# Who computes the low halves, and what VectorE does in which order, in a two-layer hybrid transformer kernel with experts

## The reference

```python
for l in range(DEPTH):                                   # DEPTH = 2
    u = rms_norm(x, norm_mix[l]) @ w_in[l]               # four mixers on slices of u, then
    y = rms_norm(stack([mla, pool, swa, conv]), ...)     # a norm by group
    x = x + y @ w_mix_out[l]
    m = rms_norm(mem, norm_mem[l])                       # 256 memory tokens
    x = x + cross_attention(rms_norm(x, norm_xa[l]), m, ...)
    x = x + hier_moe(rms_norm(x, norm_ffn[l]), ...)

def hier_moe(t):          # 4 groups of 8 experts, D_EXPERT = 256
    g_idx = argmax(g_logits)                             # one group for a token
    top_p, top_i = top_k(softmax(e_logits[rows, g_idx]), 2)   # two experts of it
    # 1024 (token, expert) pairs sorted by expert; for each expert's rows xb:
    y = (silu(xb @ w_gate[e]) * (xb @ w_up[e])) @ w_down[e]
    # y * weight is added back to its token
```

## Time and profile before

| | before |
|---|---|
| median of 3 runs | 1306.23 us (1302.16 to 1306.77) |
| the profiled execution: its time, its span | 1300.3 us, 1298.6 us |
| TensorE busy | 1185.5 us, 91% |
| VectorE busy | 702.1 us, 54% |
| ScalarE busy | 350.5 us, 27% |
| GpSimd busy | 68.8 us, 5% |
| the chain that ended last | PE 80%, DVE 11%, issue 3%, ACT 2%, DVEq 2%, DMA 1%, ACTq 1% |
| mean granted TensorE clock | 0.954 |

### The profile page before, as it was taken

One profiled execution on the slowest core, in us unless ns is written; L12 is line 12 of the kernel. 1 busy time (PEld: TensorE's weight loads), 2 busy tenths in 40 slices (PEclk: granted clock), 3 DMA queues, 4 the chain that ended last, 5 costly groups with the idle time before them and its releaser, 6 DMA issues.

```text
span 1298.6 us, 17523 instructions
## 1 busy us (share of the span) xinstructions
PE 1185.5 (91%) x5132; PEld 636.9 (49%) x5132; DVE 702.1 (54%) x1592; ACT 350.5 (27%) x737; POOL 68.8 (5%) x125
## 2 busy tenths in 40 slices
PE   5999999999396999999889998999994699999996
PEld 3754555556362444444457555555663444444443
DVE  3345664567763555555642365545766635555554
ACT  3215221124512222222232242210335122222221
POOL 8000000000206000000000000000002000000000
PEclk8999999999698999999989999989996989999999
DMA  9040024400404999999342200244013069999991
GB/s 291 18 130 1 1 65 130 195 1 2 195 0 148 421 416 418 423 421 422 153 140 66 65 1 1 66 130 195 1 40 156 0 243 409 418 422 422 419 382 65
DMA packets 52102, 243.15 MB, mean 187 GB/s; under 512 B 7872, under 2 KB 18400, under 8 KB 26944
## 3 DMA queue, kind: packets, MB, share of 16 engines
q1 hardware_dynamic: 48816, 238.30, 46.4%
q0 software_dynamic: 2688, 1.91, 0.9%
q10 hardware_dynamic: 528, 2.10, 0.4%
HBM read 240.19 MB, written 2.10 MB: 187 GB/s over the span
## 4 chain that ended last, share of the span: by engine, by line
PE 80%; DVE 11%; issue 3%; ACT 2%; DVEq 2%; DMA 1%; ACTq 1%
PE ps L2507 17%; PE ps L2117 10%; PE ps L2540 9%; PE ps L2336 8%; PE ps L2109 7%; PE ps L2491 6%; PE ps L2492 4%; PE ps L2087 4%; PE ps L2138 4%; PE ps L2384 2%; PE ps L2179 2%; PE ps L2477 1%; PE ps L2391 1%; PE ps L2187 1%; DMA X<-in_x 1%
## 5 line engine op out<-in xcount | busy, mean ns | idle before, releaser
L2507 PE MATMUL ps<-wgu,xw 128*64 128x512 f32 x1024 | 228.3, 599 | 18.8 <-ACTq L1184 17.7
L1958 DVE TENSOR_TENSOR X<-ps,X 128x512 f32<-128x512 f32 x256 | 155.9, 680 | 10.9 <-issue 9.0
L2117 PE MATMUL ps<-hT,ring 128*128 128x512 f32 x352 | 157.0, 601 | 0.0
L2507 PEld LDWEIGHTS ps<-wgu,xw 128*64 128x64 f32 x1024 | 75.6, 139 | 165.9 <-issue 165.9
L2540 PE MATMUL ps<-wdn,hhT 128*64 128x512 f32 x512 | 119.7, 610 | 2.8 <-ACTq L1202 2.8
L2336 PE MATMUL ps<-ring,yT 128*128 128x512 f32 x256 | 117.9, 609 | 0.4 <-DVE X L1361 0.4
L2491 PE MATMUL ps<-yhi,Wt 128*128 128x512 f32 x256 | 114.0, 445 | 3.7 <-DVEq L1247 3.7
L2117 PEld LDWEIGHTS ps<-hT,ring 128*128 128x128 f32 x352 | 66.6, 193 | 77.4 <-issue 77.4
L2492 PE MATMUL ps<-ylo,Wt 128*128 128x512 f32 x256 | 101.0, 394 | 0.0
L1976 DVE SCALAR_TENSOR_TENSOR ylo<-ps,ws,yhi 128x512 fp32r<-128x512 f32 x64 | 48.0, 750 | 73.5 <-ACTq L1212 73.5
L1965 DVE TENSOR_TENSOR hh<-ps,silu 128x256 f32<-128x256 f32 x32 | 13.6, 424 | 134.8 <-ACTq L1190 134.8
(11 more groups left out here) (373 smaller groups left out, 1550.4 us busy)
## 6 DMA issues: line engine op xcount, KB each, us to landing
wgu<-in_w_gate SPq DMA_DIRECT2D x64, 1024.0 KB, 8.0
wgu<-in_w_up SPq DMA_DIRECT2D x64, 1024.0 KB, 10.2
wdn<-in_w_down SPq DMA_DIRECT2D x64, 1024.0 KB, 10.6
ring<-in_w_in SPq DMA_DIRECT2D x8, 1024.0 KB, 6.7
ring<-in_w_mix_out SPq DMA_DIRECT2D x12, 512.0 KB, 5.8
w_kv<-in_xa_w_kv SPq DMA_DIRECT2D x2, 2048.0 KB, 9.5
ring<-in_w_in SPq DMA_DIRECT2D x2, 2048.0 KB, 17.1
ring<-in_w_in SPq DMA_DIRECT2D x2, 1536.0 KB, 20.2
```

The costliest lines, as they stand in the source:

```text
L1958: tt(xh, bank, xh, ALU.add).then_inc(mfreed((what, n)), 1)
L2117: last = mm(bank, w[:, c, c0:c0 + P], hT[:, c, :], start=c == 0, stop=c == KD - 1)
L2507: last = mm(bank[r], xw[:, c, r], wgu[2 * parity + j][:, :, c, :], start=c == 0, stop=c == KD - 1)
```

## The change

The diff, cut to what the text speaks of:

```diff
@@ SyncE @@
                 sp.dma_start(w_kv[:], cols("xa_w_kv", l, 0, 512)).then_inc(w_kv_in, 16)
+                with sp.If(l < 1):
+                    sp.dma_start(X[:], x_d).then_inc(x_in, 16)
@@ GpSimd @@
...
+            pool.affine_select(out=ident[:], in_=ident[:], ...)
+            pool.drain()
+            pool.nop().then_inc(ident_ready, 1)
...
-                load_gain(3, "norm_mem", gains_in)
-                load_gain(0, "norm_mix", gains_in)
...
-                for t in range(NT):
-                    wait_apart(pool, S["xhi_ready"], done(l, "xhi_ready", t + 1))
-                    pool.tensor_tensor(xlo[:, t], xs[:, t], xhi[:, t].bitcast(F32), ALU.subtract)
@@ ScalarE @@
-            act.wait_ge(mem_in, 16)
-            act.dma_start(X[:], x_d).then_inc(x_in, 16)
+            load_gains(0)
...
+                with act.If(l > 0):
+                    load_gains(l)
                 act.wait_ge(S["layer_done"], l + 1)
...
-                    chunked = X[:, t].rearrange("p (j c) -> p c j", c=KD)
-                    copy(xs[:, t].rearrange("p (c j) -> p c j", c=KD), chunked, scale=rstd_x[:, t:t + 1])
-                    copy(xhi[:, t].rearrange("p (c j) -> p c j", c=KD), chunked,
-                         scale=rstd_x[:, t:t + 1]).then_inc(S["xhi_ready"], 1)
+                    copy(xhi[:, t], X[:, t], scale=rstd_x[:, t:t + 1]).then_inc(S["xhi_ready"], 1)
...
+                act.wait_ge(S["rank_read"], done(l, "rank_read", 1))
+                copy(rt[:, 0:2].rearrange("p a b -> p (a b)")[:, 0:NT * NE + NE],
+                     ps[:, dense.job["rank",][0], 0:NT * NE + NE]).then_inc(freed(("rank",)), 1)
+                act.nop().then_inc(S["rank_kept"], 1)
@@ VectorE @@
+            def first_of(vals, n, m, code, tmp):
+                for t in range(NT):
+                    stt(tmp[:, t], vals[:, t], m[:, t:t + 1], descending[:, 0:n], ALU.is_equal, ALU.mult)
+                dve.drain()
+                nc.vector.tensor_reduce(code.unsqueeze(2), tmp, AX_X, ALU.max)
...
+                def low_part(t):
+                    dve.wait_ge(S["xhi_ready"], done(l, "xhi_ready", t + 1))
+                    stt(xlo[:, t], X[:, t], rstd_x[:, t:t + 1], xhi[:, t].bitcast(F32), ALU.mult, ALU.subtract)
+                    signal("xlo_ready")
...
                 one_hot(0, 0)
+                low_part(0)
                 one_hot(0, 1)
-                dve.nop().then_inc(S["starts_ready"], 1)
+                low_part(1)
+                ts(dest_2[:], dest[:], -float(SEQ), None, ALU.add)
+                nc.vector.tensor_copy(starts[:], row(4))
+                signal("starts_ready")
+                low_part(2)
                 one_hot(0, 2)
+                low_part(3)
                 one_hot(0, 3)
+                token_weights()
+                one_hot(1, 0)
+                sorted_gain(0)
+                one_hot(1, 1)
+                tiles_past()
+                one_hot(1, 2)
                 padded_places()
-                one_hot(1, 0)
-                one_hot(1, 1)
-                sorted_gain(0)
-                one_hot(1, 2)
                 one_hot(1, 3)
-                overflow_tiles()
-                token_weights()
                 nc.vector.memset(xgT[:, :, 2 * SEQ:SORTED], 0.0)
                 sorted_gain(1)
                 placed()
+                overflow_tiles()
                 step_(0, 0, False)
@@ TensorE @@
-            pe.wait_ge(init_pool, 1)
+            pe.wait_ge(ident_ready, 1)
...
+                pe.wait_ge(S["rank_kept"], done(l, "rank_kept", 1))
...
-                                mm(mbank_of(l, 0, ("sorted", half, c)), xhi[:, t, c * P:(c + 1) * P], hot,
+                                mm(mbank_of(l, 0, ("sorted", half, c)), xhi[:, t, c::KD], hot,
...
-                                mm(bank, xhi[:, t, c * P:(c + 1) * P], hot, start=False, stop=False)
-                            last = mm(bank, xlo[:, t, c * P:(c + 1) * P], hot, start=False, stop=t == NT - 1)
+                                mm(bank, xhi[:, t, c::KD], hot, start=False, stop=False)
+                            last = mm(bank, xlo[:, t, c::KD], hot, start=False, stop=t == NT - 1)
```

More of the change, by code:

```diff
@@ L449, in build @@
         xw = at("xw", [P, KD, P], F32, late + 4096)
+        passed = at("passed", [P, OVF, NE], F32, late + 8192)
+        begun = at("begun", [P, OVF, NE], F32, late + 10240)
         W1 = at("W1", [P, SEQ], F32, late + 12288)
@@ L483, in build @@
         past = small("past", [P, 8])
+        descending = small("descending", [P, NE])
         kTx = small("kTx", [P, 2, MEM])
@@ L502, in build @@
         ssq_q = small("ssq_q", [P, NT])
-        eps_q = small("eps_q", [P, 1])
         lg = small("lg", [P, NT, 36])
@@ L863, in square, with load_gains @@
                 return nc.scalar.activation(dst, src, ACT.Square, **kw)
-            act.wait_ge(mem_in, 16)
-            act.dma_start(X[:], x_d).then_inc(x_in, 16)
+            def load_gains(l):
+                for i, name in ((3, "norm_mem"), (0, "norm_mix")):
+                    act.dma_start(gains[:, i, :], lay(name, l).rearrange("l (p c) -> p (l c)", c=KD),
+                                  allow_slow_non_contiguous=True).then_inc(gains_in, 16)
+            load_gains(0)
             act.wait_ge(rope_arg, 1)
@@ L930, in _ @@
             with act.Fori(0, DEPTH) as l:
+                with act.If(l > 0):
+                    load_gains(l)
                 act.wait_ge(S["layer_done"], l + 1)
+                act.wait_ge(mem_in, (l + 1) * 16)
+                for i in range(NM):
+                    square(xn[:, i], memx[:, i], accum_out=mem_s[:, 0, i:i + 1])
+                    act.drain()
+                act.nop().then_inc(S["mem_ssq"], 1)
                 act.wait_ge(x_in, 16)
@@ L937, in _ @@
                 act.nop().then_inc(S["x_ssq"], 1)
-                act.wait_ge(mem_in, (l + 1) * 16)
-                for i in range(NM):
-                    square(xn[:, i], memx[:, i], accum_out=mem_s[:, 0, i:i + 1])
-                    act.drain()
-                act.nop().then_inc(S["mem_ssq"], 1)
                 normalise(l, 0)
@@ L1384, in _ @@
                 dve.sem_inc(s_, 1)
-            dve.wait_ge(init_pool, 1)
+            for j in range(16):
+                freq = float(np.float32(THETA) ** (-np.float32(j) / np.float32(16)))
+                nc.vector.memset(freqs[:, j:j + 1], freq)
+            nc.vector.memset(ovf_f[:], 0.0)
+            nc.vector.memset(ssqY[:], 1.0)
+            for w in range(4):
+                rows = slice((w % 2) * HALF, (w % 2 + 1) * HALF)
+                nc.vector.memset(inv_w[rows, w // 2:w // 2 + 1], 1.0 / WINDOWS[w])
+                nc.vector.memset(inv_n[rows, w // 2, :], float(WINDOWS[w]))
             dve.wait_ge(pos_in, 16)
@@ L1440, in _ @@
                 signal("mem_rstd")
+                stream_rstd(l, 0)
                 for t in range(NT):
@@ L1772, in _ @@
-                tt(r32(1), lg[:, :, NG:36], rstd_x[:].unsqueeze(2).to_broadcast([P, NT, NE]), ALU.mult)
+                for t in range(NT):
+                    stt(lg[:, t], lg[:, t], rstd_x[:, t:t + 1], b_rt[:], ALU.mult, ALU.add)
                 dve.drain()
-                tt(r4(0), r4(0), b_rt[:, 0:NG].unsqueeze(1).to_broadcast([P, NT, NG]), ALU.add)
-                tt(r32(1), r32(1), b_rt[:, NG:36].unsqueeze(1).to_broadcast([P, NT, NE]), ALU.add)
+                nc.vector.tensor_reduce(r1(3), groups, AX_X, ALU.max)
@@ L1846, in sorted_gain, with tiles_past @@
                         signal("xgT_dve")
-                def padded_places():
+                def tiles_past():
+                    dve.wait_ge(S["rank_kept"], done(l, "rank_kept", 1))
                     past_7 = over[:, 0:NE * 7].rearrange("p (e k) -> p e k", k=7)
@@ L1852, in padded_places @@
                        past[:, 0:7].unsqueeze(1).to_broadcast([P, NE, 7]), ALU.is_gt)
+                    nc.vector.memset(row(2), 0.0)
                     dve.drain()
@@ L1860, in padded_places @@
                     stt(row(2), row(3), float(NE - 1), iota[:, 0:NE], ALU.add, ALU.subtract)
+                def padded_places():
                     ts(r32(5), rank, float(SLOTS), None, ALU.is_ge)
```

145 lines of the change are left out of this document (60 added, 85 removed).

## The result

| | before | after |
|---|---|---|
| median (range), runs | 1306.5 us (1302.16 to 1308.18), 4 | 1268.62 us (1267.95 to 1269.59), 4 |
| span of the profiled execution | 1298.6 us | 1267.9 us |
| mean granted TensorE clock | 0.954 | 0.966 |
| first routing operation to first expert product, layer 0 / 1 | 66.24 / 66.17 us | 48.38 / 48.31 us |

The changed kernel takes 0.9719 of the time of the one before, 95% interval 0.9691 to 0.9748. It is 37.9 us faster on the medians. The forecast was 1257 us from a gain of 46.4; the time is within its range of 1246 to 1276 but 11.6 us above the forecast. On the two profiled spans only 30.7 us are seen; experiment 12 tells where the rest went.

What follows compares the result with a forecast made beforehand. The prediction took TensorE, 91% busy and waiting for VectorE in sorting, as the bound. Gains of 4.1 (start), 21.2 and 21.1 us (layers) sum to 46.4, between 1253.9 and 1259.8: 1257 us, range 1246 to 1276.

Steps and rivals of the forecast that it cites:

- GpSimd's stalls: In routing and sorting, four VectorE operations a layer are held while GpSimd uses SBUF; removing this saves 8.55 us.
- The order: VectorE evicts right behind its last G: 5.6 us less at the halves' turn, expert-step gap 3.5 instead of 9.
- M to the first product: From the matrix M to the first sorting product: 7.2 us less, of which 6.46 are stalls.
- strided weight loads taken as 0: TensorE's 256 sorting weight loads in steps of 8 elements fit beside products of 0.227 us and cost 0.
- rival A: Strided loads slow the sorting products by up to 0.095 us each, 24 us in all: 1281; chance 0.06.
- The top-two chain, "0.8 less": From the first routing operation to M: shorter scalings, top-two steps and group part save 0.8 us, besides a 2.09 stall.
- The start, 4.1 us: At the kernel's start, earlier gains and X landing at 18.7 bring the third tile to 32.3 instead of 36.41.
- The level: Whole-kernel base for the gain: profiled run 1300.3 gives 1253.9, median 1306.23 gives 1259.8; 1257 taken.
- B: VectorE's long routing operations are not GpSimd's doing, so 8.5 us stay in each layer: 1274; chance 0.06.
- D: Expert steps are bound by DMA and give back what sorting gains, 42 us: 1299; chance 0.02.
- C: The start gives nothing, X being as late behind `w_kv` as beside it: 1261; chance 0.04.
- E: Strided loads are not hidden beside sorting products, 256 times, 82 us: 1339, slower than before; chance 0.02.

Runs made afterwards that it cites:

- experiment 12: The kernel before, unaltered, profiled again: 1303.5 us, ratio 0.9993.
- experiment 3: The changed kernel with the low halves worked out by GpSimd again, from an extra copy by ScalarE: 1282.52 us, ratio 0.9833.
- experiment 4: The kernel before with only the low halves moved to VectorE and TensorE's weight loads strided; old order, chain and start kept: 1295.14 us, ratio 0.9943.
- experiment 5: The changed kernel with VectorE's old order behind the fourth low half and the overflow list in its old, longer form: 1288.62 us, ratio 0.988.
- experiment 9: The changed kernel, but GpSimd asks for its small parameters only when X has landed: 1264.82 us, ratio 0.97.
- experiment 6: The changed kernel with the old start (gains by GpSimd's queue, one constants signal, X asked for by ScalarE, X's squares first): 1272.45 us, ratio 0.9744.
- experiments 2 and 10: The changed kernel with halves laid out by chunks for contiguous weight loads: for all token tiles 1266.73 us, for tiles 1 to 3 only 1270.43 us.

## Why the prediction was right, and where it missed

The time fell within the range and the two main mechanisms held; the forecast of the gain was 8.4 us too high, and one of the prediction's own signs of being wrong, products spaced wider than 0.24, came true. The rows add up: 17.86 us from routing to experts in either layer and 2.33 at the start are 38.0, and 1306.5 - 38.0 = 1268.5, near the measured 1268.62. That it meets so closely is luck: the interval of the ratio is 3.7 us either way, and the clock in the mixers moves a profile by more. The forecast had 46.4.

- **GpSimd's stalls: right.** Put back into the changed kernel (experiment 3) they cost 7.0 and 6.9 us a layer; the held operations there begin later within GpSimd's 2.36 us than those of the earlier trace rows, whose surplus was 8.55. With only this edit (experiment 4) the gain is 4.8 and 4.1: in layer 0 about 1.6 went to the first low half, for which TensorE waited, and 2.3 to strided loads.
- **The order: right.** 8.8 and 9.2 us a layer by experiment 5, the longer list included. No wait at the turn but 0.24; the gap ahead of the expert step 3.44 us (forecast 3.5).
- **M to the first product: right**, 3.79 us where 342.4 - 338.55 = 3.85 was worked out; the low part took 1.28 us (1.4 taken), and VectorE stayed ahead. The overflow list is hidden: it begins at 384.90, beside gate and up.
- **The step that failed most, strided weight loads taken as 0.** I compared eight strided transposes with eight contiguous ones and concluded that a strided load fits. A transpose's load is not that of a sorting product: here the trace shows 330 ns against 188. There was a warning in the profile of before, in its weight loads of those transposes, which I had not read (contiguous `Prx`, then strided `X`):
```profile
L2087 PEld LDWEIGHTS ps<-ident,Prx 128*128 128x128 f32 x64 | 7.5, 143 | 1.5 <-issue 1.1
L2087 PEld LDWEIGHTS ps<-ident,X 128*128 128x128 f32 x128 | 16.2, 194 | 3.9 <-issue 2.3 <-ACT PTx L860 1.1 <-DVEq L1247 0.3
```
  The spacing of the transposes does not show these 51 ns. The half's 64 products take 0.245 x 64 = 15.7 us, not 14.5, so the two halves take 33.75 us together in layer 0 and 33.88 in layer 1 instead of the forecast 31.4: 2.4 a layer (128 x 0.018 = 2.3). This is rival A's mechanism at a fifth of its bound: 0.018 us a product and not 0.095, 4.6 us and not 24. The load is 0.14 us longer and the spacing 0.018, so the rest lies beside the product ahead. The Trainium skill's note on cachelines ("SBUF — State Buffer", section "SBUF: two separate sides"), that each access which crosses to a new 16-byte line pays a penalty, agrees with TensorE's loads in these rows, 330 ns against 188, and with VectorE's low part, 2.10 against 1.28 us. It gives no size; the 1281 that the prediction set beside it was ScalarE's loss of the earlier trace rows carried over to TensorE, and the rows show 1268.6.
- **The top-two chain, "0.8 less".** M came at 7.40 us, not at 6.3. The old chain without the stall takes 9.22 - 2.09 = 7.13, so nothing became shorter. I had taken the four short operations as 0.1 us apart; they start 0.16 apart, and four of them (0.81 to the next) replace two of 0.37, so that each top-two step is 0.08 longer and not 0.15 shorter. The four scalings take 0.82 us to the next operation instead of 0.90, 0.08 less and not 0.3, and the group's part is 0.06 shorter and not 0.23. With an instruction gap ahead of L1371, 0.2 longer than usual, that is 1.1 us a layer.
- **The start, 4.1 us.** `w_kv` landed at 13.8 and not 12.3, X at 20.56 and not 18.7. I had counted the bytes ahead and divided by a rate of 340 GB/s; GpSimd's small loads lowered the rate while X was under way. With them held back (experiment 9) X lands at 18.5, close to the forecast. Why I missed it: in the changed kernel GpSimd starts these loads at 8.67 us, and their bytes are next to nothing, though they take 9.1% of the engines' time (experiment 9's rows). Measured 2.3 us in this pair of profiles, about 2.5 over all (experiment 6).
- **The level.** 1257 lay between 1253.9, against the profiled run, and 1259.8, against the median. The profiled run met fewer low stretches than its repetition (experiment 12), so the median was the better anchor: 2.8 us of the miss. The terms make up 46.4 - 38.0 = 8.4: 2 x 2.4 for the loads, 2 x 1.1 for the chain, 1.8 for the start, less 0.4 for small terms.
- **The rivals.** B is refuted by experiment 3. D: the expert steps take as long as before, 255.92 and 251.84 us from the first expert product to the end of a layer against 254.76 and 251.36 with other draws of the clock. C is half true: X came no earlier, yet 2.3 us were gained, as the products with `w_kv` began at 13.98 instead of 16.76. E never came near: 0.018 us a load against 0.18.

## What to carry to other kernels

When two engines' operations end together again and again, look at who ends 0.15 us ahead: having the low halves on VectorE instead of GpSimd is worth 7 us a layer in the changed kernel, though it put 5 us of work on the critical engine. In the old order, without the later wait, the same move gave 4 to 5. Once that is done, the order of the queue decides: put evictions that another engine awaits ahead of everything that nobody awaits yet (9 us a layer). And price a strided operand by a row of the same instruction in the same position, with the same neighbour to hide behind; a row of another use misled me.

## What was unexpected of the hardware

- A matmul's strided weight load (steps of 32 bytes) takes 330 ns instead of 188, and slows a stream of 512-column products only from 0.227 to 0.245 us.
- The same stride in one operand costs VectorE's `scalar_tensor_tensor` of 1024 elements 0.8 to 1.0 us (2.10 to 2.28 against 1.28), so that moving the stride to VectorE loses as much as TensorE gains (experiments 2 and 10).
- While GpSimd's 2.36 us subtraction of two SBUF tensors ran, VectorE operations that read two SBUF tensors were held until it ended, whatever their size, even 128x4 (2.10 us instead of 0.16), and once a Gx, which reads one; a reduction of one tensor (0.28) and a tensor_tensor with one input in PSUM (0.29) were not. It goes both ways: in layer 1 of the kernel before, a Gx that had begun 0.04 us ahead of GpSimd's fourth subtraction took its usual 0.48, and the subtraction 2.64.
- Small loads from another queue, 0.12 MB within the first 30 us, delayed a 2 MB transfer by about 1.6 us (landing at 20.3 on the mean of eight profiles, at 18.5 and 18.9 without them); 3.8 MB of loads (544 and 384 columns of 1024 float32) behind it on its own queue delayed it by nothing.
- Four short VectorE operations in a row with a pointer for a scalar started 0.17 us apart at 36 elements (0.76 us in all), 0.16 at 32 (0.74) and 0.13 at 4 (0.62).
